# Attention with the values as left operand, a fused bias and extreme, and a recurrence step ordered by direction

## What is computed

```python
# neighbourhood attention ("na"): 8 heads, window of 8x16 positions, bias table, and all context keys
s_win = jnp.einsum('bqhd,bqkhd->bhqk', q_blk, k_win) * scale + rpb[:, rr_blk, rc_blk][None]
s_ctx = jnp.einsum('bqhd,bkhd->bhqk', q_blk, k_ctx) * scale
p = softmax_f32(jnp.concatenate([s_win, s_ctx], axis=-1))
out = p[..., :n_win] @ v_win + p[..., n_win:] @ v_ctx

# grouped attention ("gqa"): 8 query heads on 2 key/value heads, keys are all latents and the context
p = softmax_f32(jnp.concatenate([q @ k.T, q @ k_ctx.T], -1) * scale)

# the third one ("fox") is causal, with a forget bias folded into the queries and keys

# recurrence ("scan"), 8 heads of 64x64 state, forward and backward over context and latents
def step(s, inp):
    r_t, w_t, k_t, v_t, kk_t, b_t = inp
    sa = jnp.einsum('bhij,bhj->bhi', s, kk_t)
    s = s * w_t[:, :, None, :] - sa[..., None] * b_t[:, :, None, :] + v_t[..., None] * k_t[:, :, None, :]
    y = jnp.einsum('bhij,bhj->bhi', s, r_t) if emit else None
```

## Time and profile before

| | before |
|---|---|
| median of 3 runs | 4515.94 us |
| the profiled execution | 4520.69 us, its span 4518.9 us |
| mean granted TensorE clock | 0.939 |
| TensorE busy | 3995.2 us, 88% |
| VectorE busy | 1841.8 us, 41% |
| ScalarE busy | 1442.5 us, 32% |
| GpSimd busy | 698.1 us, 15% |
| na, gqa, scan, fox | 522 to 796, 796 to 1145, 1878 to 2530, 3440 to 3622 us |

### The profile page before, as it was taken

One profiled execution on the slowest core, in us unless ns is written; L12 is line 12 of the kernel. 1 busy time (PEld: TensorE's weight loads), 2 busy tenths in 40 slices (PEclk: granted clock), 3 DMA queues, 4 the chain that ended last, 5 costly groups with the idle time before them and its releaser, 6 DMA issues. The chain is left out here.

```text
span 4518.9 us, 81306 instructions
## 1 busy us (share of the span) xinstructions
PE 3995.2 (88%) x34225; PEld 3323.6 (74%) x34225; DVE 1841.8 (41%) x3182; ACT 1442.5 (32%) x3036; POOL 698.1 (15%) x551
## 2 busy tenths in 40 slices
PE   8999799799889996588898789987986978999998
PEld 2789788698679984388888434456985766888786
DVE  3224377333532125654444554565115552111234
ACT  2111155465531114533333330024114552122133
POOL 0000253110100193133333530000000000000000
PEclk9999899899899998799999889998997988999999
DMA  8233442110422376522222411233224131111121
GB/s 334 73 104 107 121 84 43 43 40 7 183 96 94 117 239 218 201 59 53 59 62 53 156 62 36 90 131 113 94 84 150 39 141 61 50 46 49 38 90 70
DMA packets 291285, 439.68 MB, mean 97 GB/s; under 512 B 76980, under 2 KB 210708, under 8 KB 286399
## 3 DMA queue, kind: packets, MB, share of 16 engines
q1 hardware_dynamic: 290664, 429.81, 29.9%
q10 hardware_dynamic: 288, 5.07, 0.3%
HBM read 315.76 MB, written 124.03 MB: 97 GB/s over the span
## 5 line engine op out<-in xcount | busy, mean ns | idle before, releaser
L387 PE MATMUL g_acc<-g_wh,l_x_high 128*128 128x320 f32 (+5 forms) x1824 | 592.3, 325 | 39.6 <-DVE g_wl L53 33.0
L387 PE MATMUL g_acc<-g_wl,l_x_high 128*128 128x320 f32 (+5 forms) x1824 | 590.4, 324 | 0.0
L387 PE MATMUL g_acc<-g_wh,l_x_low 128*128 128x320 f32 (+5 forms) x1824 | 590.3, 324 | 0.0
L387 PEld LDWEIGHTS g_acc<-g_wh,l_x_high 128*128 128x128 f32 x1824 | 346.7, 190 | 47.9 <-DVE g_wl L53 34.1
L387 PEld LDWEIGHTS g_acc<-g_wl,l_x_high 128*128 128x128 f32 x1824 | 347.1, 190 | 2.8
L387 PEld LDWEIGHTS g_acc<-g_wh,l_x_low 128*128 128x128 f32 x1824 | 346.5, 190 | 2.4
L411 ACT COPY g_o<-g_acc 128x320 f32<-128x320 f32 (+6 forms) x120 | 54.5, 454 | 769.4 <-PE g_acc L387 710.6
L435 DVE COPY g_o<-g_acc 128x320 f32<-128x320 f32 (+6 forms) x120 | 62.7, 524 | 572.3 <-PE g_acc L387 527.1
L3020 PE MATMUL ffi_acc<-l4a_x_high,ffi_wh 128*128 128x512 f32 x704 | 275.0, 391 | 12.0 <-DVE ffi_wl L53 12.0
L3020 PE MATMUL ffi_acc<-l4a_x_low,ffi_wh 128*128 128x512 f32 x704 | 274.7, 390 | 0.0
L3020 PE MATMUL ffi_acc<-l4a_x_high,ffi_wl 128*128 128x512 f32 x704 | 274.6, 390 | 0.0
(11 more groups left out here) (497 smaller groups left out, 9094.8 us busy)
## 6 DMA issues: line engine op xcount, KB each, us to landing
scan_F<-s_FE SPq DMA_DIRECT2D x160, 192.0 KB, 3.9
s_FE<-feat_f SPq DMA_DIRECT2D x10, 2304.0 KB, 7.8
ffi_w<-in_w_ffn_in SPq DMA_DIRECT2D x44, 512.0 KB, 3.8
g_cu<-s_U SPq DMA_DIRECT2D x24, 768.0 KB
pj_o<-s_O SPq DMA_DIRECT2D x26, 512.0 KB, 4.5
front_w<-in_attn_ada_w SPq DMA_DIRECT2D x8, 1536.0 KB, 11.7
front_w<-in_rec_ada_w SPq DMA_DIRECT2D x8, 1536.0 KB, 12.3
g_wr<-in_w_ffn_out SPq DMA_DIRECT2D x44, 256.0 KB, 2.6
```

Of the source, the lines that this page charges most:

```text
L387: mm = pe.matmul(acc[r][:, 0:it["n"]], left, right, start=(k == 0 and q == 0), stop=(k == kt - 1 and q == 2))
```

## The change

In attention the operands of `mix` change sides: the values of a tile are loaded (64 columns) and the transposed probabilities streamed (128 columns). Even tiles add up in the lower 64 partitions of `po`, odd tiles in the upper 64. The result is transposed and in two parts, so it is copied to SBUF (`move`, into `oT`) and multiplied once more with two stacked unit matrices (`flip`), which adds the parts and turns them back, into columns 128 to 191 of the same bank. `move` is on ScalarE in na and fox (`act_moves`), on VectorE in gqa. In gqa VectorE also takes the copy of the third group of transposes, and that group is turned before the next scores. Bias or mask, sign and extreme become one `tensor_tensor_reduce` on VectorE, for na and fox. The sums get four buffers in place of two.

In the scan GpSimd makes direction 0's mid before direction 1's near; TensorE runs step 1 of direction 0, then all output pieces of direction 0, then step 1 of direction 1; VectorE updates the state direction by direction, between the two first transposes.

```diff
-                        for t in tl:
-                            mm = pe.matmul(po[w % NPO][:, 0:HD], probT[w % 2][:, t, :], v[g % 2][:, u["tiles"][t], :],
-                                           start=(t == 0), stop=(t == len(u["tiles"]) - 1))
+                        for t in tl:
+                            half = slice(t % 2 * HD, (t % 2 + 1) * HD)
+                            mm = pe.matmul(po[w % NPO][half, 0:P], v[g % 2][:, u["tiles"][t], :], probT[w % 2][:, t, :],
+                                           start=(t < 2), stop=(t >= len(u["tiles"]) - 2))
                     mm.then_inc(summed, 1)
+                def flip(w):
+                    if w == 0:
+                        pe.wait_ge(two_out, 2)
+                    pe.wait_ge(moved, w + 1)
+                    pe.matmul(po[w % NPO][:, P:P + HD], oT[w % 2][0:halves(w), :], two[0:halves(w), :], start=True, stop=True).then_inc(flipped, 1)
...
                         turning(w - 1, (0, 1))
+                        if w >= 2:
+                            flip(w - 2)
+                        turning(w - 1, (2,))
                         if w + 1 < N:
                             score(w + 1)
-                        turning(w - 1, (2,))
                         mix(w - 1)
...
                             score(w)
+                        if w > LA:
+                            flip(w - LA - 1)
                         if w >= LA:
                             mix(w - LA)
...
                     if w >= 2:
                         act.wait_ge(trans, first[w - 1])
-                        act.wait_ge(normed, w - 1)
+                    if w >= 4:
+                        act.wait_ge(normed, w - 3)
...
+                def move(w):
+                    act.wait_ge(summed, w + 1)
+                    if w >= 2:
+                        act.wait_ge(flipped, w - 1)
+                    nc.scalar.copy(oT[w % 2][0:halves(w), :], po[w % NPO][0:halves(w), 0:P]).then_inc(moved, 1)
...
-                        dve.tensor_tensor(to[:, CTX:CTX + 640], src[:, CTX:CTX + 640], bias[h % 2][:, u["bias"], :], ALU.add).then_inc(dve_seq, 1)
-                        link.n += 1
-                        link(dve.tensor_copy(to[:, 0:CTX], src[:, 0:CTX]))
-                        src = to
-                    if causal is not None:
-                        link(dve.tensor_tensor(src[:, n - P:n], src[:, n - P:n], mask[:, :], ALU.add))
+                        dve.tensor_tensor_reduce(out=biased[w % 2][:, 0:n], in0=src[:, a:a + n], in1=add, scale=-1.0, scalar=3e38,
+                                                 op0=ALU.add, op1=ALU.min, accum_out=mx[:, w % 2:w % 2 + 1]).then_inc(maxed, 1)
+                        return
...
                     if w < N:
                         maximum(w)
-                    if w >= LA:
-                        normalize(w - LA)
+                    if w > LA:
+                        normalize(w - LA - 1)
+                    if shared and w >= LA:
+                        turn(w - LA)
+                    if not act_moves and w >= LA:
+                        move(w - LA)
+                normalize(N - 1)
...
-                pieces = {1: ((0, 0), (0, 1)), 2: ((0, 2),), 4: ((0, 3), (1, 0)), 5: ((1, 1),), 6: ((1, 2), (1, 3))}
+                pieces = {0: ((0, 0), (0, 1), (0, 2), (0, 3)), 2: ((1, 0),), 4: ((1, 1),), 5: ((1, 2),), 6: ((1, 3),)}
...
-                    for k in range(1, 8):
-                        if n < NCH:
+                    for k in range(8):
+                        if n < NCH and k < 2:
+                            step(n, 1, (k,))
+                        elif n < NCH:
                             step(n, k)
```

More of the change, by code:

```diff
@@ L615, in products, with attention_stage @@
                     mm.then_inc(self.turned, 1)
[L618 removed]
+def attention_stage(nc, name, ident, K, nk, units, heads, kv_of, q_in, k_in, v_in, o_out, LA, shared, split, table_in=None, window=None, causal=None, act_moves=False):
     SMAX = max(sum(n for _, n in u["keys"]) for u in units)
@@ L640, in attention_stage @@
         mx = st.sb("mx", [P, 2])
-        den = st.sb("den", [P, 2])
-        rden = st.sb("rden", [P, 2])
+        den = st.sb("den", [P, 4])
+        rden = st.sb("rden", [P, 4])
+        two = st.sb("two", [P, HD])
+        oT = [st.sb(f"oT{i}", [P, P]) for i in range(2)]
         o = [st.sb(f"o{i}", [P, NU, 2, HD]) for i in range(2)]
@@ L649, in attention_stage @@
             table = [st.sb(f"table{i}", [P, 18 * HD]) for i in range(2)]
-            bias = [st.sb(f"bias{i}", [P, 5, 640]) for i in range(2)]
+            bias = [st.sb(f"bias{i}", [P, 5, SMAX]) for i in range(2)]
             mask = st.sb("mask", [P, 5, 640])
+        if causal is not None:
+            mask = st.sb("mask", [P, SMAX])
+        if window is not None or causal is not None:
             biased = [st.sb(f"biased{i}", [P, SMAX]) for i in range(2)]
-        if causal is not None:
-            mask = st.sb("mask", [P, P])
-        const_in, zeroed = st.sem("const_in"), st.sem("zeroed")
+        const_in, zeroed, plain = st.sem("const_in"), st.sem("zeroed"), st.sem("plain")
         loaded = [st.sem(f"loaded{i}") for i in range(2)]
@@ L691, in has_bias, with on_vector, copied, halves @@
         def has_bias(w):
-            return window is not None and units[work[w][1]]["bias"] is not None
+            return causal is not None or (window is not None and units[work[w][1]]["bias"] is not None)
+        def on_vector(i):
+            return shared and i == 2
+        def copied(eng, n):
+            sides = [on_vector(i) for g in groups for i in range(len(g))][:n]
+            eng.wait_ge(turned, len(sides) - sum(sides))
+            if sum(sides):
+                eng.wait_ge(turned_v, sum(sides))
         def kv(h):
             return kvs.index(kv_of[h])
+        def halves(w):
+            return P if len(units[work[w][1]]["tiles"]) > 1 else HD
         def scores_done(eng, w):
@@ L737, in _ @@
                 elif causal is not None:
-                    sp.dma_start(mask[:, :], causal).then_inc(const_in, 16)
+                    sp.wait_ge(plain, 1)
+                    sp.dma_start(mask[:, SMAX - P:SMAX], causal).then_inc(const_in, 16)
                 load(1)
@@ L888, in _ @@
                 link = Linked(dve, dve_seq)
+                for hb in (slice(0, HD), slice(HD, P)):
+                    dve.tensor_copy(two[hb, :], ident[hb, hb]).then_inc(two_out, 1)
                 if not split:
@@ L892, in _ @@
                 if causal is not None:
+                    dve.memset(mask[:, :], 0.0).then_inc(plain, 1)
                     dve.wait_ge(const_in, 16)
+                if window is not None:
+                    for b in bias:
+                        dve.memset(b[:, :, 0:CTX], 0.0).then_inc(plain, 1)
                 def maximum(w):
@@ L1386, in grams, with step @@
                         mm.then_inc(s["grams"], 1)
-                def step(n, k):
-                    for d in range(2):
+                def step(n, k, ds=(0, 1)):
+                    for d in ds:
                         s, a, b = e[d], bank[d][1], bank[d][2]
@@ L1709, in _ @@
                     if n < NCH:
+                        start(n, 1)
                         for k in range(1, 8):
```

83 lines of the change are left out of this document (52 added, 31 removed).

## The result

The kernel after takes 4407.8 us, the kernel before 4515.7 (medians of runs on the same chip): a ratio of 0.976, 95% interval 0.974 to 0.978, 108 us less. I had forecast 4431, 85 less.

| stage | before, us | after, us | difference | forecast |
|---|---|---|---|---|
| na | 250.6 | 221.0 | -29.6 | -23 |
| gqa | 327.4 | 310.8 | -16.6 | -20 |
| scan | 641.1 | 579.9 | -61.2 | -43 |
| fox | 170.2 | 169.4 | -0.8 | 0 |

The account below looks back on a forecast made before the run. TensorE, busy 88% of the span, was taken as the bound. Terms -24 - 11 + 9 + 0 - 9 - 7 - 43 = -85 gave 4520.7 - 85 - 4.75 = 4431 us; own range 4395 to 4455, 8 in 10 for 4390 to 4500.

Parts of the forecast that it names:

- The value product: Attention's product with the values: a pass every 0.0545 us; full gqa unit 2.15 to 1.09 us, na 1.51 to 0.87.
- the two rivals on the halves: Value product: halves take turns, 0.109 us a pass, 4578 us, chance 0.16; partial overlap, 0.08 us, 4499 us, chance 0.08.
- Flip and shape change: Added on TensorE per attention unit: 0.22 us to turn the result back, 0.25 for both changes of the array's shape.
- The new wait: In gqa, the third group of transposes waits for ScalarE's first copy, about 0.22 us in each full unit.
- The head change: At na's changes of head, the fused VectorE step lets the exponential start 1.3 us sooner, 7 times, -9 us.
- the 7 us for the clock: In na, TensorE's slow clock stretches behind the waits at new heads go away, -7 us.
- The wait for mid: Scan: TensorE's 2.34 us gap for GpSimd's last part becomes 0.7 in the 15 chunks that emit, -25 us.
- The 0.25 expected at step 2 of direction 1: Scan: this step waits about 0.25 us for ScalarE's copy and VectorE's transpose behind the later first step.
- the five others: Scan's first five chunks, without output pieces: only the first step is drawn forward, 1 us each, -5 us.
- The step that failed: Scan: two thirds of TensorE's slow clock stretches, those of the emitting chunks, go away, -13 us.
- The copies: Rival: mix, move, flip, normalize in one row cost na and gqa 0.4 us a unit, +58, 4489 us, chance 0.10.
- A wait of the product for *normalize: Sign that the forecast is wrong: new waits of TensorE for moved or normed; no size given.

Follow-up runs that it names:

- The old table's run: Kernel after with the old table of the scan's output pieces, all else as after: 4431.4 us, ratio to before 0.982.
- the scan alone: Kernel before with the whole scan function of the kernel after, attentions untouched: 4462.8 us, ratio to before 0.988.
- the one half: Kernel after with every tile of the value product in the lower half of the result: 4568.6 us, ratio to before 1.012.
- the mids late: Kernel after with both GpSimd mids last and both first steps together behind direction 0's four pieces: 4430.8 us, ratio to before 0.979.
- the new table alone: Kernel before with only the scan's output pieces moved, four of direction 0 ahead of both first steps: 4534.7 us, ratio to before 1.003.

## Why the prediction was right, and where its sizes were off

**The value product.** 0.0545 a pass was the forecast, 0.055 came. The row it was read from, the scan's product on two quarters, carried over to halves that share their rows. No row of before showed that, and the two rivals on the halves had 0.24 together, so this part was a bet on the nearest row. Both fell with it.

**Flip and shape change.** The flip was put at 0.22; its two passes start 0.058 apart, not 0.112, and the next could follow after 0.109: 0.17. The two changes of shape were put at 0.25 and cost 0.23: from the last pass of the product to the next scores 0.20 in place of 0.055, and from the scores to the product 0.32 where it took 0.24 from the scores to the transposes before. (By the earlier trace rows the two changes there cost 0.10 and 0.14; the 0.15 that the prediction gives further down is a slip.)

**gqa.** A full unit gave 0.29 us, not 0.37. The new wait was sized at 0.22 and measures 0.40 - 0.11 = 0.29; the second transpose behind it starts 0.17 after the first in place of 0.11; the flip is 0.05 cheaper. Together that is the missing 0.08. I had also treated the wait as a price of the design, and it was only one of the order. At a change of head two things happened that the sum doesn't have: TensorE's wait for the exponential fell from 1.50 to 0.62 us, and a new one of 0.54 for *normalize* came.

**na.** A full unit went from 3.10 to 2.92 us, 0.18 for a forecast of 0.17. The head change was mis-sized: TensorE's gap there shrank from 2.40 us (2.12 and the tail) to under 0.6, more than the 1.3 forecast. From one head to the next na took 29.90 us and takes 26.55. Of these 3.35 the eight full units are some 1.4 and the fused step 1.08, 7 us in all for a forecast of 9. The rest, some 0.9, came with the other changes. The normalization no longer stands ahead of the exponential, and the sums have four buffers; which of them it was, no run isolates. Of the 7 us for the clock 5 came: before, three of the seven changes of head had a low stretch behind them, and such a head took 31.50 us; now none has. The fourth stretch stood behind na's first wait, and in the trace after the low stretch of the stage ahead reaches 8 us further there.

**Scan.** The wait for mid fell from 43.6 to 13.8 us. In each chunk with pieces that is 1.85. The 0.25 expected at step 2 of direction 1 is there as well, at 0.18: the transpose that it needs ends at 2221.27, and it starts at 2221.33, 0.23 after the pass ahead of it where 0.05 is the pace. The table of waits doesn't show it, since it is shorter than the tail. So these chunks gained 1.67 each, forecast 1.65: this step was right. In the five others I had put 1.0, though the first step of 0.47 is all that could fill that hole, and it shrank by 0.46. The size came out all the same, by a wait that I hadn't seen. Step 2 of direction 0 waited for its transpose there before, and with the early first step it doesn't:

```profile
2024.80 0.68 PE L1349 MATMUL scan_bank<-scan_M,scan_SS 64*64 64x64 f32 x16 [0.74 <-DVE scan_SS L1651]
```

0.46 + 0.74 - 0.18 makes 1.0. That is luck.

The step that failed is the clock's: I left a third of the low stretches to the five chunks without pieces, and all 12 went, 40.8 us at half speed, 20.4 for 13. The old table's run shows that holes of 1.72 us, the size left in those five chunks, brought none in 19 cases. That isn't certain for a single hole: of the other traces with the new scan, two have one low stretch each among the first five chunks, the scan alone and the one half. The last 11 us of the 61 are smaller waits that I had not put in, among them TensorE's for the transposes (8.2 to 4.9, the 0.74 above included) and gaps with no releaser.

**Fox** came out at nothing, as forecast. **The copies** (*move*, *turn*) held nobody up for long. A wait of the product for *normalize*, a sign I had named as wrong, did come in gqa, but only nine times, at short units, 0.54 us at most and 4.7 in all. (That rival's price counts 144 units; na and gqa have 160.)

**In all** the prediction was 23 us short: 18 of them in the scan, the clock's 7 and the 11 of waits not put in, and 7 in na, against 3 too many in gqa.

## What to carry to other kernels

If a product leaves half of the array's columns free, give successive tiles to the two halves and turn the sum back once at the end; count the cost of turning back before the gain, since a unit of two tiles has little to halve. Fill a wait for another engine with work whose inputs you have first made ready: the pieces moved alone made the kernel slower, and beside the new orders of VectorE and GpSimd they were worth 20 us. After a change has made one step shorter, look at orders around it again, as the next wait may be one that a swap of two lines removes.

## What the runs showed of the hardware

Each half of the array's columns takes its passes from the queue on its own, and started up to four passes ahead of its turn (the two runs with the even tiles first). With two passes of each half in turn the 20 passes of a full gqa unit start within 1.04 us, with four and four within 1.09, with ten and ten within 1.75, and all in one half within 2.12.

TensorE's clock stood at its lower level for 3.4 us behind 12 of the 20 holes of 2.18 us before (2.45 from the last start to the next), and behind 4 of the 5 such holes with the mids late. Behind the 19 holes of 1.72 us (1.94 from start to start) with the old table it never did. In the kernel after and seven more traces with the same scan, each with four such holes and one of 1.49, it did so twice: once behind the hole of 1.49 in the first chunk, and once behind one of 1.72 with one of 1.48 6 us later. With the new table alone, where five holes are 2.18 us and 15 are 3.05, there were 15 low stretches, three of them of 6.8 us.

A float32 pass on a quarter or a half of the array starts every 0.058, 0.109 and 0.218 us for 64, 128 and 256 streamed columns where 64 are loaded. On the whole array with 128 columns loaded it starts every 0.109 for 128 streamed ones, and every 0.112 for 64.

VectorE's fused add, sign and extreme takes 1.09 us for 128x896, as long as the reduction alone (1.08), and 0.08 to read the accumulator.
